# Queries of the latent attention: six full tiles in place of eight padded ones, rotary rows carried to their heads by DMA

## The reference, cut to what matters

```python
def apply_rope(x, cos, sin):
    half = x.shape[-1] // 2
    x1, x2 = x[..., :half], x[..., half:]
    return concatenate([x1 * cos - x2 * sin, x2 * cos + x1 * sin], axis=-1)

c_q = rms_norm(q_lat, mla_q_norm)                       # 512 x 256
q_m = (c_q @ w_q_b).reshape(B, S, 8, 96)
q_m = concatenate([q_m[..., :64], apply_rope(q_m[..., 64:], cos_m, sin_m)], axis=-1)
k_rope = apply_rope(kv_lat[..., 128:].reshape(B, S, 1, 32), cos_m, sin_m)   # one for all heads
k_m = concatenate([kv[..., :64], broadcast(k_rope, 8 heads)], axis=-1)
o_m = softmax attention(q_m, k_m, v_m, scale = 96 ** -0.5)
```

## Time and profile before

| | |
|---|---|
| median of three runs | 2311.42 us (2309.55 to 2312.17) |
| profiled execution, its own time | 2312.75 us |
| its span, first to last instruction | 2310.8 us |
| TensorE busy | 2276.3 us, 99% of the span |
| DVE busy | 1323.8 us, 57% |
| ACT busy | 882.1 us, 38% |
| GpSimd busy | 218.3 us, 9% |
| mean granted clock of TensorE | 0.998 of full speed |

### The profile page before, as it was taken

One profiled execution on the slowest core, in us unless ns is written; L12 is line 12 of the kernel. 1 busy time (PEld: TensorE's weight loads), 2 busy tenths in 40 slices (PEclk: granted clock), 3 DMA queues, 4 the chain that ended last, 5 costly groups with the idle time before them and its releaser, 6 DMA issues.

```text
span 2310.8 us, 28465 instructions
## 1 busy us (share of the span) xinstructions
PE 2276.3 (99%) x10956; PEld 1639.3 (71%) x10956; DVE 1323.8 (57%) x2063; ACT 882.1 (38%) x1522; POOL 218.3 (9%) x183
## 2 busy tenths in 40 slices
PE   9999999999999999999999999999999999999998
PEld 7756876443775587634377788888888778888887
DVE  5676645233667564523367657777335665877722
ACT  5475542211447554212142334444223234444422
POOL 0212201000221220100000020000001002000000
PEclk9999999999999999999999999999999999999999
DMA  5301558999430145899963223333333423333331
GB/s 185 95 2 46 189 215 332 410 409 410 166 99 6 46 164 215 333 410 409 410 235 109 74 91 101 95 97 100 95 97 137 115 68 92 102 99 100 101 89 57
DMA packets 112662, 381.63 MB, mean 165 GB/s; under 512 B 16528, under 2 KB 17296, under 8 KB 112272
## 3 DMA queue, kind: packets, MB, share of 16 engines
q1 hardware_dynamic: 108928, 367.05, 45.3%
q0 software_dynamic: 2304, 8.39, 0.9%
q10 hardware_dynamic: 1296, 4.37, 0.5%
HBM read 363.51 MB, written 6.29 MB: 160 GB/s over the span
## 4 chain that ended last, share of the span: by engine, by line
PE 88%; DVE 5%; ACT 3%; DMA 2%; issue 1%; POOL 1%; SPq 0%; POOLq 0%; DVEq 0%; ACTq 0%
PE ps L1394 11%; PE ps L1396 11%; PE ps L1395 11%; PE ps L1701 9%; PE ps L1418 5%; PE ps L1419 5%; PE ps L1420 5%; PE ps L1723 5%; PE ps L1582 3%; PE ps L1438 3%; PE ps L1437 3%; PE ps L1439 3%; PE ps L1532 2%; PE ps L1540 2%; DMA wa<-in_wu 1%; PE ps L1733 1%
## 5 line engine op out<-in xcount | busy, mean ns | idle before, releaser
L2534 DVE TENSOR_TENSOR wlo<-stage,whi 128x1024 fp32r<-128x1024 f32 x262 | 328.3, 1257 | 268.0 <-ACT whi L1846 267.2
L1394 PE MATMUL ps<-hTh,whi 128*128 128x512 f32 x1120 | 441.0, 394 | 0.1
L1396 PE MATMUL ps<-hTh,wlo 128*128 128x512 f32 x1120 | 436.3, 390 | 0.0
L1395 PE MATMUL ps<-hTl,whi 128*128 128x512 f32 x1120 | 436.0, 389 | 0.0
L1846 ACT ACTIVATE whi<-stage 128x1024 fp32r<-128x1024 f32 x262 | 276.0, 1057 | 324.6 <-PE ps L1420 120.6
L1394 PEld LDWEIGHTS ps<-hTh,whi 128*128 128x128 f32 x1120 | 210.3, 188 | 48.2 <-issue 4.7
L1396 PEld LDWEIGHTS ps<-hTh,wlo 128*128 128x128 f32 x1120 | 210.2, 188 | 44.0
L1395 PEld LDWEIGHTS ps<-hTl,whi 128*128 128x128 f32 x1120 | 210.4, 188 | 42.6
L2446 DVE TENSOR_TENSOR ps<-ps,Rs 128x512 f32<-128x512 f32 x124 | 86.1, 698 | 140.0 <-PE ps L1396 126.0
L2449 DVE SCALAR_TENSOR_TENSOR t<-ps,vecs,t 128x511 f32<-128x511 f32 (+1 forms) x176 | 131.1, 745 | 3.7 <-ACT t L1803 0.7
L2446 DVE TENSOR_TENSOR x<-x,ps 128x512 f32<-128x512 f32 x184 | 116.5, 682 | 28.4 <-PE ps L1420 18.0
(11 more groups left out here) (387 smaller groups left out, 4255.6 us busy)
## 6 DMA issues: line engine op xcount, KB each, us to landing
stage<-in_wpk SPq DMA_DIRECT2D x268, 512.0 KB, 3.6
wa<-in_wd SPq DMA_DIRECT2D x56, 512.0 KB, 15.5
wa<-in_wu SPq DMA_DIRECT2D x54, 512.0 KB, 15.1
wa<-in_wg SPq DMA_DIRECT2D x46, 512.0 KB, 14.4
ws<-in_wg SPq DMA_DIRECT2D x26, 512.0 KB, 13.5
ws<-in_wu SPq DMA_DIRECT2D x24, 512.0 KB, 12.0
wr<-in_wg SPq DMA_DIRECT2D x24, 512.0 KB, 15.2
stage<-in_wd SPq DMA_DIRECT2D x22, 512.0 KB, 16.4
```

The source lines that it names most:

```text
L1394: pe.matmul(o, h, ah, start=k == 0, stop=False)
L1395: pe.matmul(o, h, al, start=False, stop=False)
L1396: t = pe.matmul(o, lo, ah, start=False, stop=k == 7)
L2534: ve.tensor_tensor(M.wlo[i % NW][:, :], M.stage[i % NSTAGE][:, :], f(M.whi[i % NW][:, :]), ALU.subtract).then_inc(*S.wlo.mark(("w", i)))
```

## The change

The 768 query columns are packed without padding. When a chunk of these weights (numbers 10, 11, 48 and 49, the list LATQ) is rounded, ACT and DVE write it in two instructions each: first the plain columns of all heads, 512, then the rotary ones, 256. Four tiles (mq) then hold the plain columns of two heads each; ACT copies one head's half, DVE the other's. Two tiles (mqr) hold the rotary columns of four heads each, and they come first. DVE multiplies such a tile by the cosine into `lc` and by the sine into `ls`, both 128 x 512, and SP moves each head's 32 rows of either to `mq`, eight DMAs of 32 x 512 per tile. Since the query no longer has its halves swapped, the key is swapped instead: two DMAs of 16 x 512 take the place of ACT's copy. The sine table `sin4` is loaded by eight DMAs of 16 x 512 at each mixer's start, the cosine table `cos4` by four DMAs of 32 x 512 in place of one. tick() is called after tiles 1, 3 and 5.

```diff
@@ Order.mixer
         ready = self.head(ns, s)
+        self.do("sines", l)
...
-        for h in range(8):
+        for t in range(6):
             u = self.take()
-            self.do("mq", l, h, u, i0, i1)
+            self.do("mq" if t > 1 else "mqr", l, t - 2 if t > 1 else t, u, i0, i1)
             self.drop(u)
-            if h in (1, 4, 7):
+            if t in (1, 3, 5):
                 self.tick()
@@ TensorE
-                hh, ll = (w[i % NW][:, h * 128:(h + 1) * 128] for w in (M.whi, M.wlo))
+                hh, ll = (w[i % NW][:, r] for w in (M.whi, M.wlo))
@@ ACT, rounding of a weight chunk (DVE's wlo likewise)
+            if i in LATQ:
+                w, x = M.latq(M.whi[i % NW]), M.latq_in(M.stage[i % NSTAGE])
+                ac.activation(w[0], x[0], ACT.Copy).then_inc(*S.whi.mark())
+                ac.activation(w[1], x[1], ACT.Copy).then_inc(*S.whi.mark(("w", i)))
+                continue
...
-        elif name == "krope":
-            l = a[0]
-            q.wait_ge(*S.dve.at("krope", l))
-            copy(M.krope[96:128, :], M.krope[64:96, :], ("krope", l))
@@ SP
+        elif name == "sines":
+            l, = a
+            if l:
+                all_before(q, S, "mixer", l)
+            for g in range(4):
+                for h in range(2):
+                    r = slice(32 * g + 16 * h, 32 * g + 16 * h + 16)
+                    sp.dma_start(M.sin4[r, :], M.dram["rope1"][2][112 - 16 * h:128 - 16 * h, :]).then_inc(
+                        *S.sines.mark(("sines", l)))
+        elif name == "krope":
+            l = a[0]
+            q.wait_ge(*S.dve.at("krope", l))
+            for h in range(2):
+                o, r = slice(96 + 16 * h, 112 + 16 * h), slice(80 - 16 * h, 96 - 16 * h)
+                sp.dma_start(M.krope[o, :], M.krope[r, :]).then_inc(*S.kswap.mark(("krope", l)))
+        elif name == "mqr":
+            l, t, *_ = a
+            q.wait_ge(*S.dve.at("mqr", l, t))
+            for g in range(4):
+                r = slice(32 * g, 32 * g + 32)
+                sp.dma_start(M.mq[64:96, 4 * t + g, :], M.lc[t][r, :]).then_inc(*S.mqr[t].mark(("mqr", l)))
+                sp.dma_start(M.mq[96:128, 4 * t + g, :], M.ls[t][r, :]).then_inc(*S.mqr[t].mark(("mqr", l)))
@@ DVE
-            stt(M.mq[64:128, h, :], M.ps[u[0]][64:128, :], 96 ** -0.5, M.mcs[64:128, :], ALU.mult, ALU.mult, ("mq", l, h),
-                ("free",) + u)
+            ts(M.mq[0:64, 2 * p + 1, :], M.ps[u[0]][64:128, :], 96 ** -0.5, ALU.mult, ("mq", l, p), ("free",) + u)
+        elif name == "mqr":
+            l, t, u, i0, i1 = a
+            q.wait_ge(*S.pe.at("mqr", l, t))
+            q.wait_ge(*S.sines.at("sines", l))
+            stt(M.lc[t][:, :], M.ps[u[0]][:, :], 96 ** -0.5, M.cos4[:, :], ALU.mult, ALU.mult)
+            stt(M.ls[t][:, :], M.ps[u[0]][:, :], 96 ** -0.5, M.sin4[:, :], ALU.mult, ALU.mult, ("mqr", l, t), ("free",) + u)
```

More of the change, by code:

```diff
@@ L1068, in __init__ @@
         self.sing = at("sing", OC + 1408 + 2 * KB, [128, 512])
-        self.mcs = at("mcs", OC + 1408 + 4 * KB, [128, 512])
+        self.cos4 = at("cos4", OC + 1408 + 4 * KB, [128, 512])
+        self.sin4 = A("sin4", 54 * KB, [128, 512])
+        self.lc = [A(f"lc{t}", (68 + 4 * t) * KB, [128, 512]) for t in range(2)]
+        self.ls = [A(f"ls{t}", (70 + 4 * t) * KB, [128, 512]) for t in range(2)]
         oc = OC + 1408 + 6 * KB
@@ L1486, in pe_program @@
                 q.wait_ge(*S.dve.at("lo", ("cq", l), k))
-                hh, ll = (w[i % NW][:, h * 128:(h + 1) * 128] for w in (M.whi, M.wlo))
+                hh, ll = (w[i % NW][:, r] for w in (M.whi, M.wlo))
                 pe.matmul(o, hh, ah, start=k == 0, stop=False)
                 pe.matmul(o, hh, al, start=False, stop=False)
-                t = pe.matmul(o, ll, ah, start=False, stop=k == 1)
-            t.then_inc(*S.pe.mark(("mq", l, h), ("w", i0), ("w", i1)))
+                last = pe.matmul(o, ll, ah, start=False, stop=k == 1)
+            last.then_inc(*S.pe.mark((name, l, t), ("w", i0), ("w", i1)))
         elif name == "mk":
@@ L1918, in act_program @@
         elif name == "mq":
[L1919 to L1921 removed]
+            l, p, u, i0, i1 = a
+            q.wait_ge(*S.pe.at("mq", l, p))
+            copy(M.mq[0:64, 2 * p, :], M.ps[u[0]][0:64, :], ("mq", l, p), ("free",) + u, scale=96 ** -0.5)
         elif name == "mk":
@@ L1959, in act_program @@
                     q.wait_ge(*S.mk[m].at("mk", l))
+            elif kind == "mix" and g == 1:
+                for m in range(2):
+                    q.wait_ge(*S.mqr[m].at("mqr", l))
             copy(PT[g % len(PT)][:, :, qt * 128:(qt + 1) * 128],
@@ L2533, in dve_program @@
                 q.wait_ge(*S.pe.at("e", i // 38 - 1, 177))
+            if i in LATQ:
+                w, x, h = M.latq(M.wlo[i % NW]), M.latq_in(M.stage[i % NSTAGE]), M.latq(M.whi[i % NW])
+                ve.tensor_tensor(w[0], x[0], f(h[0]), ALU.subtract).then_inc(*S.wlo.mark())
+                ve.tensor_tensor(w[1], x[1], f(h[1]), ALU.subtract).then_inc(*S.wlo.mark(("w", i)))
+                continue
             ve.tensor_tensor(M.wlo[i % NW][:, :], M.stage[i % NSTAGE][:, :], f(M.whi[i % NW][:, :]),
@@ L3077, in __init__ @@
         self.mk = [signal(f"key_rope{p}", 16) for p in range(4)]
+        self.mqr = [signal(f"query_rope{t}", 16) for t in range(2)]
+        self.sines, self.kswap = signal("sines_in", 16), signal("key_swap", 16)
         self.dup = [signal(f"key_dup{g}", 16) for g in range(2)]
```

34 lines of the change are left out of this document (22 added, 12 removed).

## The result

| | before | changed |
|---|---|---|
| median | 2311.80 us (2309.55 to 2312.62, 4 runs) | 2326.25 us (2324.06 to 2327.95, 4 runs) |
| ratio, 95% interval | | 1.0061 (1.0049 to 1.0073) |
| span of the profiled execution | 2310.8 us | 2322.2 us |
| time of the profiled execution | 2312.75 us | 2324.06 us |

The changed kernel is slower by 0.6%, 14.45 us between the medians and 11.4 us between the two profiled spans. The profiled execution was the shortest of its four. The forecast was 2324, with 2318 to 2331.

A forecast was written before the change was run, and what follows sets the result against it. Attention's start was taken to hang on the chain of SP's swap DMAs and DVE, not TensorE. Delays of 6.5 + 6.0 = 12.5 us put the profiled run at 2325.2, the median at 2324 us, range 2318 to 2331.

The forecast's parts named there:

- The queue: SP, layer 0: sixteen issues of 0.61 us, 9.7 us in all, ahead of sq1's swap, which goes out 6.5 us later.
- The waits of TensorE: Layer 0: idle 2.5 us before the turn near 90, and from about 96.5 to 101.9 before the second value tile.
- The saving buys nothing: 24 removed matmuls, at most 5.5 us, gain nothing because TensorE waits at both places.
- the saving shows: Rival: TensorE alone sets the time, so 24 fewer matmuls save 5.5 us, giving 2306; chance 0.06.
- From sq1 to the attention: Layer 0: sq1 at 99.6, sq2 at 107.2, row maximum at 108.7, first turn at 110.4, 6.5 us later.
- The clock: Rival: TensorE's idle 5.4 us per mixer lowers its clock, at most +2.9 us per mixer, 2324 to 2330; chance 0.12.
- Cheap queue: Rival: sixteen issues hold SP under 3.3 us, so sq1's swap goes out as before, 2311; chance 0.08.
- The sum: Both mixers: 6.5 us in layer 0 plus 6.0 in layer 1, 12.5 us slower.
- The small prices: Sine loads, swapped-key DMAs and two-piece weight rounding: nothing lost; sines issued at 0.61 us each, wanted at 38.49.

The follow-up runs named there:

- e2: The kernel before, keeping its eight query tiles, plus sixteen filler DMAs of 32 x 512 at the same place in SP's queue; 2325.67 us, ratio 1.0062.
- e5: The changed kernel with its sixteen DMAs spread by pairs of heads: four ahead of sq1's swap, four before sq2's, eight behind; 2310.45 us, ratio 0.9995.
- e8: e5 with the rotary key's copies put behind the first doubling of the grouped key on SP; 2310.43 us, ratio 0.9994.
- e6: e5 with the turns of q1 and q2 later on DVE and the rotary key's copies behind the grouped key's first doubling; 2308.35 us, ratio 0.9984.
- e9: e6 with the second pair's four DMAs behind sq2's swap and ACT making both halves of the plain query copies; 2305.15 us, ratio 0.9972.
- e4: The changed kernel plus 24 unused matmuls ahead of the first latent value tile in each mixer, to keep the clock up; 2325.17 us, ratio 1.0060.
- e1: The changed kernel with its sixteen rotary-row DMAs replaced by two carrying the same number of bytes; 2316.44 us, ratio 1.0023.

## Why the prediction was right

*The queue.* It held: issues from 86.27 (forecast 86.0) to 96.76 (95.8). The term was short by 0.8 us in layer 0 and 0.4 in layer 1, where sixteen issues took 10.06 us. The step from one issue to the next is 0.63. The forecast's 0.61 was 2.44 / 4, which leaves out the gap behind the fourth issue: from 82.90 to the next DMA at 85.44 are 2.54 us, again 0.63 each. The rest is the one gap of layer 0. e2 shows that the DMAs in the queue make a loss of this size without the rest of the change, and e5 that the loss goes with their order.

*The waits of TensorE.* Forecast were 2.5 us before the turn near 90 and 5.4 us before the values; the trace has 1.85 and 6.37. The first was too high because the turn's row factor was to come 0.1 to 0.3 us later and came 0.4 earlier within the stage: DVE's copy starts at 89.36 where it stood at 89.21, in a stage that starts 0.53 later.

*The saving buys nothing.* It held nearly. TensorE waits at both places, as forecast. But beside e2, which has the queue's delay and no saving, the changed kernel's stages are 1.8 us shorter, and in e8, with the queue in order and DVE's order as it was, they are 2.65 us shorter than before's (193.98 for 196.63), of the 5.5 that the matmuls are worth. Both are below what the times can tell. What more of it needed was named in the rival "the saving shows": that DVE is not last. e6 and e9 go towards that step by step.

*From sq1 to the attention.* sq1 came at 100.70 where 99.6 was forecast, and sq2 at 106.86 where 107.2 was. The step between them was mis-sized: I took over the 5.3 us from the scaling's end to sq2 of before. Here it is 3.9 (102.97 to 106.86), and DVE does not wait for the DMA at all but goes on from the key copies. Two errors, +1.1 and -1.4, cancel. The row maximum at 108.38 (forecast 108.7) and the turn at 110.11 (110.4) are right partly for that reason. Scores were to start at 104.0 and started at 106.68: 1.1 us because the scaling ended later, the rest because most of the values ran at half clock.

*The clock.* The rival's mechanism came true in both mixers: the granted clock was 0.50 from 100 to 106, and from 688 to 692 in layer 1. Its price didn't. In layer 0 the scores, slowed, end just as the exponential is ready: it starts at 109.11, the turn of before came 0.93 us after that (102.95 to 103.88), and here the turn stands at 110.11, within 0.1 of it. In layer 1 it still waits 0.22 us for ACT. By e4 the fall cost nothing that can be measured here. That is a near thing and partly luck: in e2, with one value tile more behind the wait, some 0.7 us were felt in layer 0. The Trainium skill, "TensorE: Matmul & The Clock Gate", section "HAM oscillation — how this bites in real kernels", foretells the fall in idle gaps. The trace agrees in the fall.

*Cheap queue.* It fell. No issue in the stretch took under 0.5 us.

*The sum.* 6.5 + 6.0 = 12.5 was forecast. Counted within each stage, the turn came 5.7 + 6.4 = 12.1 us later, so layer 0 was 0.8 too high and layer 1 0.4 too low, and a part of the near hit is that these cancel. The rest of the span was 0.8 shorter, with no term in the forecast. The profiled execution took 2324.06 where 2325.2 was forecast for it. The median lies 2.2 us above that execution, while I had set it 1.3 us below, as it was for the kernel before. That, and no term of the sum, is why 2326.25 is above 2324; nothing was run on what sets it. The low end of the range, 2318, does not follow from the price that it names: issues of 0.51 us give 2311.4 + 9.3 = 2320.7.

*The small prices.* The sines were issued at 0.46 us each (eight in 3.66 us) and DVE used them at 39.02, not waiting for them. The two-piece rounding, costed at nothing, takes DVE 1.02 us for a chunk of layer 0 (77.45 to 78.47), where one piece took 1.22.

## What to carry to other kernels

When an edit adds DMAs on an engine that issues them in order, count issues times the spacing of that shape, and look for what stands next in that queue; what waits for it pays, however few bytes move. Before pricing removed work by its own duration, follow the waits of its stage back: work that is removed from an engine which then waits buys little (here 1.8 to 2.7 of 5.5 us, in the traces) until the chain that it waits for is shortened as well. DMAs can be put off in such a queue to where their reader still gets them in time, one semaphore for each reader. When a gain is smaller than the spread of the times, the length of its stage between two matmuls that both kernels have is the steadier measure, and says nothing of the rest.

## What was not expected of the hardware

- A small DMA that was issued on time arrived 2.9 us later than usual (6.7 for 3.8 us from its first issue to its use) behind two transfers of 512 KB (e1). The two larger DMAs freed the issuing engine there and not the path.
- In both e2 and the changed kernel the sixteen issues stand some 0.63 us apart although each is shown as 0.59 long. In the changed kernel's layer 0 one gap of 0.45 us stands among them (91.85 to 92.30), which layer 1 does not have. What makes it was not looked into.
- Idle for 6.37 us, TensorE was at 1.2 GHz from 100 on and still there until 106, though it worked without a pause from 103.02; idle for 1.85 us before the turn at 89.83, it kept the full clock (1.00 from 86 to 92).
